# Per-engine loops over column chunks written as hardware loops instead of unrolled Python loops

## What is computed

```python
# block 1
h = rms_norm(x, swa_norm)
q, k, v, gate = split(h @ w_in)            # 2048 | 256 | 256 | 2048 columns
s = q @ k.T * 64**-0.5 + t5_bias            # window of 128 keys, 32 heads on 4 kv heads
p = exp(s - m) / (sum(exp(s - m)) + exp(sink - m))
x = x + ((p @ v) * silu(gate)) @ w_out
# block 2 (16 meta rows ahead of the 512)
hn = _rmsnorm(h, attn_norm_w[l])
a_q, a_k, a_v, a_g, b_cq, b_ckv, b_kr, b_g = split(hn @ w_in[l])
oA = _diff_attention(qA, kA, vA, lam, slopes)       # softmax 0 - lam * softmax 1
oB = _mla_attention(q_nope, q_pe, k_nope, k_pe, vB) # from w_uq, w_ukv projections
h = h + concat([oA * silu(a_g), oB * silu(b_g)]) @ w_out[l]
y = _rmsnorm(h, final_norm_w)
```

## Time and profile before

| what | value |
|---|---|
| median of 3 executions | 1743.61 us (1743.54 to 1745.85) |
| profiled execution, its own time | 1743.54 us |
| its span, first to last instruction | 1741.7 us, granted clock 0.996 |
| PE busy | 1693.3 us (97%) |
| POOL, ACT, DVE busy | 802.6 (46%), 699.0 (40%), 606.5 (35%) |
| instructions in the profile | 21709 |
| DMA | 187.57 MB, mean 108 GB/s |

### The profile page before, as it was taken

How to read it: one execution, slowest core, us unless ns; L and a number is a source line. 1 busy time by engine, 2 the same in 40 slices (tenths; PEclk the granted TensorE clock), 3 DMA queues, 4 the chain that set the end, 5 groups by cost and what they waited for, 6 DMA issues and landing times.

```text
span 1741.7 us, 21709 instructions
## 1 busy us (share of the span) xinstructions
PE 1693.3 (97%) x8465; PEld 1384.1 (79%) x8465; DVE 606.5 (35%) x1520; ACT 699.0 (40%) x1530; POOL 802.6 (46%) x590
## 2 busy tenths in 40 slices
PE   7999999999999999999999999999999999999995
PEld 6888797888888888898787787888866767878884
DVE  4356657663111322221100002423154344562222
ACT  3336565565333333343312245444444444333221
POOL 3462424334555454554344345433353635655552
PEclk9999999999999999999999999999999999999998
DMA  5441213212222343432233337423321312233333
GB/s 197 134 121 50 73 51 96 74 49 73 97 97 100 123 144 134 146 123 95 74 121 98 120 129 258 125 88 118 103 96 62 110 55 80 90 121 121 121 121 120
DMA packets 95953, 187.57 MB, mean 108 GB/s; under 512 B 5515, under 2 KB 12748, under 8 KB 95708
## 3 DMA queue, kind: packets, MB, share of 16 engines
q1 hardware_dynamic: 70028, 134.86, 23.7%
q10 hardware_dynamic: 20784, 36.75, 6.5%
q0 software_dynamic: 5040, 14.59, 2.8%
HBM read 161.23 MB, written 24.95 MB: 107 GB/s over the span
## 4 chain that ended last, share of the span: by engine, by line
PE 87%; DVE 7%; issue 2%; POOL 2%; ACT 2%; DMA 0%; POOLq 0%; DVEq 0%; ACTq 0%
PE acc L435 23%; PE acc L437 22%; PE acc L436 22%; PE sc L690 4%; PE turn L530 3%; PE turn L716 2%; PE turn L457 2%; POOL r_q L1189 1%; PE turn L518 1%; PE sc L448 1%; PE sc L449 1%; PE turn L704 1%; PE turn L717 1%; PE sc L505 1%; PE sc L506 1%
## 5 line engine op out<-in xcount | busy, mean ns | idle before, releaser
L1183 POOL TENSOR_TENSOR w_lo<-w_raw,w_hi 128x512 fp32r<-128x512 f32 x481 | 678.4, 1414 | 845.2 <-ACT w_hi L806 835.4
L435 PE MATMUL acc<-w_hi,setA_hi 128*128 128x512 f32 (+1 forms) x1344 | 544.9, 405 | 6.8 <-issue 5.2
L806 ACT ACTIVATE w_hi<-w_raw 128x512 fp32r<-128x512 f32 x481 | 301.3, 628 | 593.7 <-PE acc L437 583.1
L437 PE MATMUL acc<-w_hi,setA_lo 128*128 128x512 f32 (+1 forms) x1344 | 521.7, 388 | 0.0
L436 PE MATMUL acc<-w_lo,setA_hi 128*128 128x512 f32 (+1 forms) x1344 | 520.7, 387 | 0.0
L435 PEld LDWEIGHTS acc<-w_hi,setA_hi 128*128 128x128 f32 x1344 | 253.3, 188 | 62.8 <-issue 16.7
L437 PEld LDWEIGHTS acc<-w_hi,setA_lo 128*128 128x128 f32 x1344 | 252.8, 188 | 53.3
L436 PEld LDWEIGHTS acc<-w_lo,setA_hi 128*128 128x128 f32 x1344 | 253.9, 189 | 40.5
L435 PE MATMUL acc<-w_hi,setB_hi 128*128 128x512 f32 x512 | 201.3, 393 | 0.0
L437 PE MATMUL acc<-w_hi,setB_lo 128*128 128x512 f32 x512 | 199.5, 390 | 0.0
L436 PE MATMUL acc<-w_lo,setB_hi 128*128 128x512 f32 x512 | 199.3, 389 | 0.0
(11 more groups left out here) (260 smaller groups left out, 1936.1 us busy)
## 6 DMA issues: line engine op xcount, KB each, us to landing
w_raw<-in_w_in SPq DMA_DIRECT2D x48, 1024.0 KB, 5.1
w_raw<-in_swa_w_in SPq DMA_DIRECT2D x36, 1024.0 KB, 5.2
w_raw<-in_swa_w_out SPq DMA_DIRECT2D x16, 1024.0 KB, 5.1
w_raw<-in_w_out SPq DMA_DIRECT2D x16, 1024.0 KB, 5.0
bias<-row_d ACTq DMA_DIRECT2D x16, 256.0 KB, 5.1
x_in<-in_x ACTq DMA_DIRECT2D x4, 1024.0 KB, 5.1
x_d<-stage ACTq DMA_DIRECT2D x4, 1024.0 KB, 4.2
kv_d<-stage ACTq DMA_DIRECT2D x4, 1024.0 KB, 8.5
```

Source lines behind the costliest of these rows:

```text
L435: mm(acc[t][:, 0:cols], hi[:, kc, rows], wh, start=(k == 0), stop=False)
L437: last = mm(acc[t][:, 0:cols], lo[:, kc, rows], wh, start=False, stop=(k == K - 1))
L806: nc.scalar.activation(w_hi[:, f % 4], w_raw[:, q % 2, f % 4], ACT.Copy).then_inc(s_hi, 1)
L1183: nc.gpsimd.tensor_tensor(w_lo[:, f % 4], w_raw[:, (f // 4) % 2, f % 4], w_hi[:, f % 4].bitcast(F32), ALU.subtract).then_inc(s_lo, 1)
```

## The change

- PE: g (3), three loops of 3 chunks (2 each), MLA (1), differential (1), last projection (2): 13.
- ACT: g (3), three loops of 3 (2 each), MLA (1), last projection with `range(2)` (1): 11. The two differential bodies stay written out.
- DVE: g (3), two loops of 3 (2 each), MLA (1), differential (1), last (2): 11.
- POOL: g (3), three loops of 3 (2 each): 9. The attention bodies and the last six chunks stay written out.
- SP: five loops of 4 chunks (3 each), three loops of 2 (1 each): 18.

```diff
             def load_chunk(w, col, q0, quads=(0, 1, 2, 3), odd=0):
 
                 for q, rows in enumerate(quads):
+                    col_ = sp.snap(col) if not isinstance(col, int) else col
                     sp.wait_ge(s_lo, 4 * (q0 + q) + 4)
-                    sp.dma_start(w_raw[:, (q + odd) % 2], w[:, rows, :, col:col + CW]).then_inc(s_raw[(q + odd) % 2], 16)
+                    sp.dma_start(w_raw[:, (q + odd) % 2], w[:, rows, :, bass.ds(col_, CW)]).then_inc(s_raw[(q + odd) % 2], 16)
...
-            for i in range(4):
+            with sp.Fori(0, 4) as i:
                 load_chunk(w_in, i * CW, i * 4 + 4)
...
-            for g in range(4):
+            with pe.Fori(0, 4) as g:
                 for H in range(32):
                     for t in (0, 1) if H % 2 == 0 else (2, 3):
                         project(g * KC + (2 * KC + H // 2), g + 2, H // 2, t, setA_hi, setA_lo)
...
-            for i in range(2):
+            with pe.Fori(0, 2) as i:
                 attend_body(MLA, i, Q_BASE, 26)
...
             def split_hi(n0, i, k):
 
                 f = n0 + k + AHEAD
-                if f + i * KC >= PIECES:
+                if isinstance(i, int) and f + i * KC >= PIECES:
                     return
...
-                cols = slice(col, col + CW)
+                cols = slice(col, col + CW) if isinstance(col, int) else bass.ds(act.snap(col), CW)
                 act.wait_ge(s_evac, 4 * c + 8)
                 act.dma_start(dst[0:S, :].rearrange("(t p) c -> p t c", p=P)[:, :, cols], src[:]).then_inc(signal, 16)
...
-            for g in range(4):
+            with act.Fori(0, 4) as g:
...
-                        flat, heads = row_d.rearrange("h q m -> h (q m)"), slice(g * GROUP, (g + 1) * GROUP)
+                        flat, heads = row_d.rearrange("h q m -> h (q m)"), bass.ds(act.snap(g * GROUP), GROUP)
...
             def x1_hi(c, f):
+                if isinstance(c, int):
+                    dst = setA_hi[:, 4 * c + f]
+                else:
+                    dst = setA_hi[:, bass.ds(c * 4 + f, 1)].rearrange("p o s -> p (o s)")
                 act.wait_ge(s_gain_c, c + 1)
-                turn_hi(c * 4 + (32 + f), f % 2, setA_hi[:, 4 * c + f], gain_c[:, f:f + 1])
+                turn_hi(c * 4 + (32 + f), f % 2, dst, gain_c[:, f:f + 1])
...
-            for g in range(4):
+            with pool.Fori(0, 4) as g:
...
-            for g in range(4):
+            with dve.Fori(0, 4) as g:
                 link.base, link.n = g * BODY + start, 0
...
-                V.tensor_tensor(dst, stage[:], w_final[:, c * CW:(c + 1) * CW].unsqueeze(1).to_broadcast([P, NT, CW]),
+                V.tensor_tensor(dst, stage[:], w_final[:, bass.ds(c * CW, CW)].unsqueeze(1).to_broadcast([P, NT, CW]),
```

More of the change, by code:

```diff
@@ L403, in _ @@
                 sp.dma_start(w_raw[:, q % 2, 2:4], w_ukv[:, :, (2 * j + 1) * CW:(2 * j + 2) * CW]).then_inc(s_raw_2nd[j], 16)
-            for i in range(2):
+            with sp.Fori(0, 2) as i:
                 load_chunk(w_in2, i * CW, i * 4 + 81, odd=1)
-            for i in range(2):
+            with sp.Fori(0, 2) as i:
                 load_chunk(w_in2, i * CW + 4928, i * 4 + 89, odd=1)
-            for i in range(2):
+            with sp.Fori(0, 2) as i:
                 load_chunk(w_in2, i * CW + 3072, i * 4 + 97, odd=1)
-            for i in range(4):
+            with sp.Fori(0, 4) as i:
                 load_chunk(w_out2, i * CW, i * 4 + 105, quads=[k // 4 for k in ORDER[::4]], odd=1)
@@ L552, in og_turn @@
                 last = turn4(g * 4 + (16 + f), f % 2, [stage[:, t, f * P:(f + 1) * P] for t in range(NT)])
-            for i in range(3):
+            with pe.Fori(0, 3) as i:
                 for k in range(KC):
@@ L914, in gate_sigmoid @@
                 nc.scalar.activation(work[:], stage[:], ACT.Sigmoid).then_inc(s_silu, 1)
-            for i in range(3):
+            with act.Fori(0, 3) as i:
                 for k in range(KC):
@@ L1097, in attend_body @@
                     store(i + c0, dst, i * CW)
-            for i in range(2):
+            with act.Fori(0, 2) as i:
                 attend_body(MLA, i, Q_BASE, 26, 3, qa_d)
@@ L1215, in _ @@
                         root(r_q[:, cols], ss_q[:, cols], 16, g * 2 + (ROOT_Q + H - 1))
-            for i in range(3):
+            with pool.Fori(0, 3) as i:
                 for k in range(KC):
@@ L1483, in _ @@
             start2 = link.n
-            for i in range(3):
+            with dve.Fori(0, 3) as i:
                 link.base, link.n = i + start2, 0
@@ L1516, in residual @@
                 after(dve, V.tensor_tensor(ss_1[:], ss_1[:], ss_c[:], ALU.add))
-                V.tensor_copy(gain_c[:], gain_2[:, 4 * c:4 * c + 4]).then_inc(s_gain_c, 1)
+                if isinstance(c, int):
+                    last = V.tensor_copy(gain_c[:], gain_2[:, 4 * c:4 * c + 4])
+                else:
+                    last = V.tensor_copy(gain_c[:], gain_2[:, bass.ds(c * 4, 4)])
+                last.then_inc(s_gain_c, 1)
                 dve.wait_ge(s_gain_c, c + 1)
@@ L1521, in x1_lo @@
                 for f in range(4):
-                    turn_lo(c * 4 + (32 + f), f % 2, setA_lo[:, 4 * c + f], setA_hi[:, 4 * c + f], gain_c[:, f:f + 1])
+                    if isinstance(c, int):
+                        lo, hi = setA_lo[:, 4 * c + f], setA_hi[:, 4 * c + f]
+                    else:
+                        lo, hi = (s_[:, bass.ds(c * 4 + f, 1)].rearrange("p o s -> p (o s)") for s_ in (setA_lo, setA_hi))
+                    turn_lo(c * 4 + (32 + f), f % 2, lo, hi, gain_c[:, f:f + 1])
             after(dve, V.memset(ss_1[:], 0.0))
             start3 = link.n
-            for i in range(3):
+            with dve.Fori(0, 3) as i:
                 link.base, link.n = i * 2 + start3, 0
@@ L1664, in _ @@
                 first = link.n
-                for i in range(2):
+                with dve.Fori(0, 2) as i:
                     link.base, link.n = i * body + first, 0
```

13 lines of the change are left out of this document (7 added, 6 removed).

## The result

The changed kernel takes 1772.99 us (median of 4, 1770.45 to 1773.27), the kernel before 1743.74 us beside it (median of 4); the ratio is 1.0161, 95% interval 1.0146 to 1.0175. It is slower by 29 us, outside the range given.

The account below looks back on a forecast made before the run. PE's matmul stream was taken as the bound. 1741.7 + 0 (loop ends) + 5 (register work) + 1 (code fetch) = 1747.7 us of span, plus 1.9 = 1749.6 us, 0.34% slower; range 1741.5 to 1768.

Parts of the forecast that it names:

- What bounds the kernel: Whole kernel: PE's matmul stream, busy 97% of 1741.7 us; other engines count only if they reach PE through a wait.
- The step that failed: DVE's loop end in g: 2.4 us between its sequencer's last separate wait and the next g's first copy, cost 0.
- The upper bound of 4 us: Code fetch at a branch back: packet 1.2 us plus smallest landing 2.7 us, at most some 4 us together.
- PE's loop ends: Branches back on PE's sequencer, which runs 3.8, 0.9 or 1.5 us ahead of the weight loads: 0 us in the sum.
- PE's code fetch: At PE's 13 loop ends, the branch leaves its code packet: 1 us taken, between 0 and 14 us.
- the bound of 14 us: PE's code fetch at 4 us each: eight plain loop ends leave 1.6 us uncovered, five in attention 12.5 us.
- rule of the 2-page window: A taken branch to a target outside the current 2-page window forces a DMA fetch: 1762.7 us or more.
- The rival of the fetch: Each loop end fetches its code anew: 1762.7 us at a 4 us wait, 1784 at 5 us; chance 0.18.
- Register work: Added register instructions for waits and addresses: 0 in plain stages, 5 us in attention chains, between 0 and 39 us.
- crossing of a unit: Attention unit's chain crosses six times between PE, DVE and ACT; one crossing a unit later by 35 to 51 ns.
- The faster rival: Another spacing of transfers and POOL's and DVE's work removes some of PE's 15.2 us idle: at best 1738; chance 0.08.

## Why the prediction was wrong

*What bounds the kernel* was right: nothing counted until it reached PE through a wait, and four of five stretches didn't move.

*The step that failed* is "On DVE the tight one is g … 2.4 us of cover … I put it at 0". Three things were wrong in it, and the runs show each.

- The cover wasn't there. In the earlier trace rows DVE's sequencer is through its last separate wait at 181.5 us, 2.4 ahead of the first copy, because the last `o_nat`'s own wait rides on that instruction and the sequencer goes on. In the loop the count is in a register, and the trace has the wait on a register instruction of the sequencer, right ahead of `o_nat`:

```profile
L1437 DVEq FUSED_REGOPS  x1: 57/57/57, 184.9 to 184.9; - x1
```

The sequencer so reached the branch at 185.2, 0.1 us after `o_nat` had begun. I had written that "where a wait now ends a sequencer stands rather than a queue", for the units, and didn't apply it to this loop end, further up. Even without any fetch, the branch then costs 0.35 us on DVE's path (0.56 against 0.21).
- The fetch was priced for PE. The upper bound of 4 us fits the first block (2.8 to 3.1 us). It has no term for the second, 9.0 to 10.1 us after the branch, and a path that goes on after one instruction pays for that one.
- The question was put as whether a branch back leaves its packet, and answered for 16 KB packets and PE. What decides on DVE is how many blocks the body touches, three or four, and ten positions (100 and 110) make the difference.

Measured in place of 0: 27.9 us alone, 29 in the whole change.

*PE's loop ends: right, the price slightly low.* In the plain loop L583 and in g:

```profile
L583 PEldq COMPARE_BRANCH  x3: 76/208/208, 665.7 to 756.6; - x3
...
L535 PEldq COMPARE_BRANCH  x4: 76/212/238, 183.3 to 438.2; - x4
```

A branch taken costs 207 to 238 ns over the 13, not taken 76, where I had 150 with the addition. The next load follows with no gap on the matmuls.

*PE's code fetch: right at its low end.* 0 us against 1, and the bound of 14 us was empty. Between 200 and 433 us no packet of PE's queue arrives, though a g has some 900 matmuls and loads, 3.5 packets (I had written two to three for an attention body). The Trainium skill's rule of the 2-page window (Runtime: NRT & Kernel Launch, Instruction fetch mechanics), by which the prediction had each of these 13 loop ends stall, is not borne out: none fetched. On DVE a rule of this kind fits, with other numbers: four blocks of 128 instructions.

*The rival of the fetch* had the right mechanism and, at 5 us a fetch, the right loop ("DVE's in g … reaches `q_turn` too"), but spread most of its 40 us over PE's loop ends and units. Its sign of truth, gaps at the loop ends of plain stages, did not come.

*Register work: 5 us forecast.* 0.3 us, which is inside the noise, for everything but DVE's g (1739.56 against 1739.29), up to 4.0 us with it (1742.30 against 1738.31). The size was near by chance; the place was wrong. No crossing of a unit became later for the matmuls: their waits of the earlier trace rows came out the same in number and length. What is shown of the price, 2.2 us, stands at the ends of g.

*The faster rival* was right in kind, and I had dismissed it with "nothing in the change aims there": another spacing of POOL and DVE took 3.1 us off, once DVE's g was out of the way. Its mechanism, a copy that waits for POOL, is in the profile before, as a copy of two elements with a mean of 248 ns. Nothing in the profile before told which way such a shift goes: with DVE's g looped as well, 16 copies are long in place of 4.

## What to carry to other kernels

Before a long body becomes a hardware loop, count its instructions for each engine, find where its head falls in the blocks, and look for the engine whose first instruction after the branch is on the critical path. Give the branch a hint, or write that one engine's loop out; the other engines' loops here were free. The hint left the kernel 2.3 us over the one before (1746.80 against 1744.49), the loop written out put it 3.1 us under. A cover read from a wait with a constant is not there once the count is in a register: take the time at which the last waited-for event comes, and lay the branch behind that.

## What the runs showed of the hardware that was not expected

- DVE's sequencer holds a body of 278 instructions in three blocks of 128, and loses it in four unless the branch is hinted; lost, its target is usable after 2.8 to 3.1 us and the block behind it only after 9.0 to 10.1 us. Why the second packet starts 6.0 to 6.9 us after the first, when each takes 0.3 to 0.6 us, stays open. In that time a weight load of 1 MB and four loads of `bias` are on the DMA engines (2.1 MB from 184 to 197 us in the changed kernel, busy throughout from 188 to 194). That the packet waits behind them is a possible cause that no run tested; at the entry of the loop with its head at 0, with the weight load alone, the second packet came 5.0 us after the first.
- Entering the loop by a branch (head at position 0) cost 2.8 us once with a fetch, at 98.8 us, and was hidden; falling into it cost a pause of 0.5 us.
- The branch takes 38 to 68 ns on ACT, POOL, SP and DVE of the changed kernel (up to 84 on DVE with the hint) and on PE 207 to 238 ns taken, 76 not taken.
- A two-element copy on DVE took 0.17 or 1.27 us by whether it began before or after a `w_lo` of POOL, and 0.16 us each time with its source in PSUM. A shift of tenths of a us by an unrelated edit was therefore worth 3 us of the whole, half of what was forecast for the change.
